# Four layer norms of a two-block network, computed half by half of the tokens, and a modulation sum moved to PSUM

## What is computed

```python
def second_block(x, c, ...):
    cond = jax.nn.silu(c)
    for l in range(2):
        mod = (cond @ ada_w[l] + ada_b[l])[:, None, :]
        sh_m, sc_m, g_m, sh_f, sc_f, g_f = jnp.split(mod, 6, axis=-1)
        h = x * (1.0 + sc_m) + sh_m
        y = even_mixer(h, ...) if l % 2 == 0 else odd_mixer(h, ...)
        x = layer_norm_2(DN_ALPHA * x + (1.0 + g_m) * y, ln_mix_g[l], ln_mix_b[l])
        h = x * (1.0 + sc_f) + sh_f
        y = conv_ffn(h, ffn_w_up[l], ffn_conv_w[l], ffn_w_down[l])
        x = layer_norm_2(DN_ALPHA * x + (1.0 + g_f) * y, ln_ffn_g[l], ln_ffn_b[l])
    return x

def layer_norm_2(x, g, b):
    mu = jnp.mean(x, axis=-1, keepdims=True)
    var = jnp.mean(jnp.square(x - mu), axis=-1, keepdims=True)
    return (x - mu) * lax.rsqrt(var + 1e-5) * g + b
```

## Time and profile before

| | us |
|---|---|
| median of 3 runs (2568.92 to 2570.44) | 2570.07 |
| the profiled execution's own time | 2565.9 |
| its span, first to last instruction | 2564.1 |
| PE busy in the span | 2471.4 (96%) |
| DVE, ACT, POOL busy | 1483.6, 1041.7, 1069.9 |

### The profile page before, as it was taken

The page is one execution under the profiler, slowest core; times in us unless marked ns, Lnnn a source line. Parts: engine busy times, 40 slices in busy tenths (PEclk is TensorE's granted clock), DMA queues, the critical chain, the costliest instruction groups (busy, mean ns, idle before and its releaser), DMA issues.

```text
span 2564.1 us, 30477 instructions
## 1 busy us (share of the span) xinstructions
PE 2471.4 (96%) x11318; PEld 1947.3 (76%) x11318; DVE 1483.6 (58%) x1904; ACT 1041.7 (41%) x1387; POOL 1069.9 (42%) x358
## 2 busy tenths in 40 slices
PE   7989999999999999999999998999998998999997
PEld 4658888887676788888876876888886756788886
DVE  6975756764455567477537775651654365652553
ACT  5564322235556642222434253532344343542333
POOL 5844444434343434444343423444435212444443
PEclk9999999999999999999999999999999999999999
DMA  5215545533222255465243312223323122224322
GB/s 147 67 58 164 186 148 183 181 91 114 83 58 75 61 178 181 145 192 169 86 129 99 99 50 74 83 78 111 98 75 98 58 70 66 72 78 121 94 78 67
DMA packets 397551, 273.37 MB, mean 107 GB/s; under 512 B 10067, under 2 KB 379731, under 8 KB 397436
## 3 DMA queue, kind: packets, MB, share of 16 engines
q1 hardware_dynamic: 383612, 221.52, 30.2%
q10 hardware_dynamic: 13824, 50.34, 5.3%
HBM read 269.70 MB, written 2.12 MB: 106 GB/s over the span
## 4 chain that ended last, share of the span: by engine, by line
PE 82%; ACT 5%; POOL 5%; DVE 4%; issue 3%; SPq 0%; DMA 0%; ACTq 0%; DVEq 0%; POOLq 0%
PE ps L688 25%; PE ps L690 25%; PE ps L689 25%; POOL act L2212 2%; POOL weight_lo L2175 2%; PE ps L1287 1%; ACT weight_hi L2310 1%; DVE act L1776 1%; PE ps L928 1%; PE ps L902 1%; PE ps L890 1%; PE ps L887 1%; ACT arena L2579 0%; DVE tmp L1604 0%; PE ps L1002 0%
## 5 line engine op out<-in xcount | busy, mean ns | idle before, releaser
L2175 POOL TENSOR_TENSOR weight_lo<-weight_raw,weight_hi 128x2048 fp32r<-128x2048 f32 (+2 forms) x223 | 917.4, 4114 | 1325.4 <-ACT weight_hi L2310 1323.5
L688 PE MATMUL ps<-u_hi,weight_hi 128*128 128x512 f32 x2312 | 915.9, 396 | 39.2 <-DVE u_lo L1395 29.2
L690 PE MATMUL ps<-u_hi,weight_lo 128*128 128x512 f32 x2328 | 910.5, 391 | 0.0
L689 PE MATMUL ps<-u_lo,weight_hi 128*128 128x512 f32 x2312 | 904.1, 391 | 0.0
L2310 ACT ACTIVATE weight_hi<-weight_raw 128x2048 fp32r<-128x2048 f32 (+2 forms) x223 | 381.3, 1710 | 543.2 <-PE ps L690 509.4
L688 PEld LDWEIGHTS ps<-u_hi,weight_hi 128*128 128x128 f32 x2312 | 436.9, 189 | 156.4 <-DVE u_lo L1395 35.1
L690 PEld LDWEIGHTS ps<-u_hi,weight_lo 128*128 128x128 f32 x2328 | 439.6, 189 | 92.9
L689 PEld LDWEIGHTS ps<-u_lo,weight_hi 128*128 128x128 f32 x2312 | 437.0, 189 | 92.7 <-issue 3.3
L688 PE MATMUL ps<-act_hi,weight_hi 128*128 128x512 f32 x704 | 274.3, 390 | 2.0 <-DVE act_lo L1361 2.0
L689 PE MATMUL ps<-act_lo,weight_hi 128*128 128x512 f32 x704 | 273.9, 389 | 0.0
L690 PE MATMUL ps<-act_hi,weight_lo 128*128 128x512 f32 x704 | 273.9, 389 | 0.0
(11 more groups left out here) (318 smaller groups left out, 2496.0 us busy)
## 6 DMA issues: line engine op xcount, KB each, us to landing
weight_raw<-in_ffn_w_up SPq DMA_DIRECT2D x132, 512.0 KB, 5.2
arena<-in_ada_w ACTq DMA_DIRECT2D x96, 512.0 KB, 5.8
weight_raw<-in_ffn_w_down SPq DMA_DIRECT2D x64, 704.0 KB, 4.7
weight_raw<-in_ffn_w_gate SPq DMA_DIRECT2D x44, 512.0 KB, 4.0
weight_raw<-in_ev_w_in SPq DMA_DIRECT2D x10, 1024.0 KB, 5.4
weight_raw<-in_conv_w_pw SPq DMA_DIRECT2D x16, 512.0 KB, 5.5
weight_raw<-in_ple_w_gate SPq DMA_DIRECT2D x16, 512.0 KB, 3.8
weight_raw<-in_attn_w_qkv SPq DMA_DIRECT2D x16, 512.0 KB, 5.2
```

The costliest lines, as they stand in the source:

```text
L688: pe.matmul(bank, w[0], x[0], start=start, stop=False)
L689: pe.matmul(bank, w[0], x[1], start=False, stop=False)
L690: return pe.matmul(bank, w[1], x[0], start=False, stop=stop)
L2175: pool.tensor_tensor(w_lo[r][:, 0:width], raw[r][:, 0:width], w_hi(k0 + j)[:, 0:width].bitcast(F32), ALU.subtract).then_inc(w_ready, 1)
```

## The change

1. **The last two tiles ahead of a seam** are computed by halves of 256 tokens (`token_halves`): tile 6 first half, tile 7 first half, tile 6 second half, tile 7 second half. The first half's statistics (`mean_stat`, `variance_stat`: three fp32 matmuls with ones on 256 tokens each) stand within tile 6's second half. The running sums end with chunk 5 instead of chunk 6.
2. **The layer norm** is done for the first 256 tokens and then for the others, on ACT, DVE and POOL, by instructions of half the width (`seam`). The second half's mean, root and table loads are put between the first half's operand chunks.
3. **The first two slots behind a seam** are computed half by half (`behind_seam`): for each half and each chunk, 12 matmuls on 256 tokens, for all four tiles. The second half's statistics stand behind chunks 0 and 1 of the first half. `fill` goes.
4. The high parts of these two slots get buffers of their own (`behind_hi`, in `arena`), so that they can be split before the seam; POOL makes both low parts ahead of centring. Slot 2 is split within the second half's operands.
5. ACT's `conv_taps` takes its first step out of the loop (`peel=1`); its tap copies then need no table load there.
6. At seam 3 the output leaves in 16 DMAs of 256 tokens instead of 8 of 512.
7. The modulation sum is kept in PSUM banks 6 and 7: two instructions of 512 for each of 1024, and two transposes for each.

```diff
-        ada_acc = arena[:, 0:D]
+        ada_acc = [ps[:, 6], ps[:, 7]]
...
+            def mean_stat(s, z):
+                cols = HALVES[z]
+                if z:
+                    pe.wait_ge(mean_neg, 2 * s + 1)
+                    pe.wait_ge(mean_free, s + 1)
+                pe.wait_ge(half_sums, s + 1)
+                pe.matmul(ps[:, 4, cols], ones, sum1[:, cols], start=True, stop=False)
+                for c in (DC - 2, DC - 1):
+                    if z == 0:
+                        pe.wait_ge(h_half, 2 * s + c - (DC - 3))
+                    else:
+                        pe.wait_ge(tile_used, BANKS + stages[SEAMS[s]][2] + c + 1)
+                    mm = pe.matmul(ps[:, 4, cols], ones, chunk(h, c)[:, cols], start=False, stop=c == DC - 1)
+                mm.then_inc(stat_half, 1)
...
+            def token_halves(s, w_of, x, kc):
...
+                def part(j, z, bank):
+                    cols = HALVES[z]
+                    for k in range(kc):
+                        hi, lo = x(k)
+                        mm = product(bank[:, cols], w_of(j, k), (hi[:, cols], lo[:, cols]), k == 0, k == kc - 1)
+                        if (j, z) == (0, 1):
+                            if k == 4:
+                                mean_stat(s, 0)
+                            if k == 6:
+                                variance_stat(s, 0)
+                    return mm
...
+            def behind_seam(name, behind=None):
...
+                order = [(j, k) for k in range(DC) for j in range(2)]
+                for z, cols in enumerate(HALVES):
+                    for at, (j, k) in enumerate(order):
+                        if j == 0:
+                            pe.wait_ge(x_half, 16 * s + 8 * z + k + 1)
...
+                        for i in range(2):
+                            mm = product(banks[j][i][:, cols], cols_of(w[j], i, k), (hi[:, cols], lo[:, cols]), k == 0, k == DC - 1)
+                            if z and k == DC - 1:
+                                mm.then_inc(tile_done, 1)
+                        if z == 0 and at == 1:
+                            mean_stat(s, 1)
+                        if z == 0 and at == 3:
+                            variance_stat(s, 1)
...
+                half_add(DC - 2, 0)
+                half_add(DC - 1, 0)
+                variance(0)
+                half_add(DC - 2, 1)
+                centre(0)
+                dve.wait_ge(root_half, 2 * s + 1)
+                scale(0, 0)
+                if mixer:
+                    first_low(0)
+                else:
+                    scale(1, 0)
+                half_add(DC - 1, 1)
+                for c in range(1 if mixer else 2, DC):
+                    scale(c, 0)
+                    if mixer and 2 <= c <= 4:
+                        low(c - 1, 0)
+                variance(1)
+                if mixer:
+                    for c in range(4, DC):
+                        low(c, 0)
+                centre(1)
+                dve.wait_ge(root_half, 2 * s + 2)
...
-                    if s == 0 and kk == 0:
-                        ada_link(dve.tensor_scalar(acc, ada_slot[kk], by, None, ALU.mult))
-                    else:
-                        ada_link(dve.scalar_tensor_tensor(acc, ada_slot[kk], by, acc, ALU.mult, ALU.add))
+                    for z, acc in enumerate(ada_acc):
+                        row = ada_slot[kk][:, z * S:(z + 1) * S]
+                        if s == 0 and kk == 0:
+                            ada_link(dve.tensor_scalar(acc, row, by, None, ALU.mult), 1 - z)
+                        else:
+                            ada_link(dve.scalar_tensor_tensor(acc, row, by, acc, ALU.mult, ALU.add), 1 - z)
...
+                for c in range(DC):
+                    operand(c, 0)
+                    if c == 0:
+                        square(DC - 1, 1)
+                    if c == 2:
+                        mean(1)
+                    if c == 3:
+                        ln_table_ahead()
+                    if c == 5:
+                        root(1)
+                for c in range(DC):
+                    operand(c, 1)
+                    if c == 3:
+                        split(next_slot + 2)
...
-                run_steps(sc, HC, body, 4, tail=2)
+                run_steps(sc, HC, body, 4, peel=1, tail=2)
```

More of the change, by code:

```diff
@@ L52 @@
 SLOT = 2048
+HALVES = (slice(0, S // 2), slice(S // 2, S))
+SEAMS = ("e_out", "down2b", "o_out", "down3b")
+BEHIND = {"up2a": 0, "o_in": 1, "up3a": 2}
 PARAM_WIDTHS = [
@@ L141, in plan_slots @@
     hi_free, last_use = [], [0] * HI_RING
+    apart = {stages["wo"][0] + 2} | {stages[name][0] + j for name in BEHIND for j in range(2)}
     for k in range(len(loads)):
-        third_wo = k == stages["wo"][0] + 2
-        hi_free.append(0 if third_wo else last_use[k % HI_RING])
-        if split_no[k] and not third_wo:
+        hi_free.append(0 if k in apart else last_use[k % HI_RING])
+        if split_no[k] and k not in apart:
             last_use[k % HI_RING] = tiles_after[k]
@@ L777, in stage_gemm @@
                 first = 2 if fill else 1
-                rest(name, body, (last if drain else last + 1) - first, first)
+                seam = SEAMS.index(name) if name in SEAMS else None
+                rest(name, body, (last if drain or seam is not None else last + 1) - first, first)
                 if drain:
                     drained()
+                if seam is not None:
+                    w = slot_of(name, Step(last))
+                    token_halves(seam, lambda i, k: cols(w, i, k), xu, DC)
             def rest(name, body, count, first=1):
@@ L808, in body @@
                     mm.then_inc(tile_done, 1)
-                run_steps(pe, DC, body, 4)
+                if seam is None:
+                    run_steps(pe, DC, body, 4)
+                    return
+                for j in range(DC - 2):
+                    body(Step(j))
+                w = [slot_of(name, Step(j)) for j in (DC - 2, DC - 1)]
+                token_halves(seam, lambda j, k: halves(w[j], lambda t: t[:, k * P:(k + 1) * P]),
+                             lambda k: (chunk(act_hi, k), chunk(act_lo, k)), HC)
             def rms_stat(adds=9):
@@ L1258, in _ @@
             stage_gemm("e_out", order=(4, 5, 6, 7, 0, 1, 2, 3))
[L1259 to L1263, removed]
+            behind_seam("up2a")
+            stage_down("down2a")
+            stage_gemm("up2b", wait=False)
+            stage_down("down2b")
             def lat_stats(chunks):
@@ L1320, in _ @@
             stage_gemm("o_out")
[L1321 to L1324, removed]
-            residual_stat("down3b")
-        operand_at = []
+            behind_seam("up3a")
+            stage_down("down3a")
+            stage_gemm("up3b", wait=False)
+            stage_down("down3b")
+            mean_stat(3, 1)
+            variance_stat(3, 1)
         @block.vector
```

381 lines of the change are left out of this document (256 added, 125 removed).

## The result

| | before | changed |
|---|---|---|
| median of the runs | 2569.49 (4 runs, 2564.89 to 2570.44) | 2603.29 (4 runs, 2598.08 to 2603.48) |
| profiled execution / span | 2565.9 / 2564.1 | 2598.1 / 2596.3 |
| PE, DVE, ACT, POOL busy | 2471.4, 1483.6, 1041.7, 1069.9 | 2492.2, 1493.8, 1065.7, 1068.8 |

A forecast was written before the change was run, and what follows sets the result against it. PE was taken as the bound, busy 2471.4 of 2564.1 us. Seams 0 and 2 (+1.5, +1.6), clock (+3.4), seam 1 (-2.0) and seam 3 (+0.9) gave +5.4 on 2570.07: 2575, with 8 in 10 from 2563 to 2584.

The forecast's parts named there:

- Nothing waits so far: Seam 0, tile 6's start to tile 7's second half ending at 14.1 us: PE meets no wait.
- Splits and DMAs of slots 0 and 1 are earlier and off the path: First two slots behind a seam: making them earlier costs nothing; only 0.48 us for `weight_lo` was waited there before.
- The third rival: More low clock and late slot 3, if DVE's multiplication slows beside POOL: 2583; chance 0.17, shared with small-operand cost.
- The half matmuls: PE at the seams: 0.120 us apart, 6.7 ns more per half; 1.9 us at seams 0 and 2, 2.2, 0.9.
- Statistics: PE at each seam: twelve fp32 matmuls on 256 columns make 5.2 us, against 3.4 for the four before.
- first operand's wait: Seams 0 and 2, after tile 7's second half: PE waits 1.8 us, 7.1 before; none at seam 1.
- new wait at slot 2: Seams 0 and 2: PE waits 3.3 us for the release of the bank of slot 0's first tile.
- the middle waits: Within the two slots behind a seam: PE's small waits for operand chunks, 3.4 us at seam 0, 3.3 at seam 1.
- The clock: Behind slot 2's wait at seams 0 and 2: 3.4 us at half clock, costing 1.7 us each.
- The 1.8 like the second: Seams 0 and 2: the 1.8 us idleness, like an earlier one of 1.7 us, is followed by no low clock.
- Seam 1: Interval to the end of slots 0 and 1: no first wait, 47.4 us plus some 0.8 against 50.3, -2.0 rounded.
- seam 3: From tile 6's start to the span's end: 33.0 us against 32.1, +0.9, through the first half's leftovers in ACT's queue.

The follow-up runs named there:

- e1: Changed kernel, but at seams 0 and 2 the gated product of a tile is written back into its own PSUM bank instead of SBUF: 2590.04 us, ratio 1.0076.
- e6: Changed kernel with a separate buffer for the last slot's high part (down2b, down3b); PE waits for slot 7 only at tile 7's first half: 2585.62 us, ratio 1.0067.
- e7: Changed kernel with the edits of e1 and e6 together: 2578.69 us, ratio 1.0027.
- e9: e7, and DVE does both shifted taps of a slot's first tile and frees its bank before turning to the second: 2573.6 us, ratio 1.0019.
- e11: e9 with DVE's second centring and chunk 0 scaling earlier, and ACT splitting slot 2 during its wait for the first variance: 2564.56 us, ratio 0.999.

## Why the prediction was wrong

- **"Nothing waits so far"** (seams 0 and 2) is the first step that failed. It took DVE's adds at their undisturbed 0.69 us and "Splits and DMAs of slots 0 and 1 are earlier and off the path" as free. The split is; POOL's two low parts that follow it, 9.6 us, aren't, since they hold DVE's add. Price: 3.04 us of wait and 1.7 us of low clock at each seam, of which e1 took back 54.0 - 49.2 = 4.8 at seam 0 and 54.1 - 49.5 = 4.6 at seam 2. The third rival had DVE slowed beside POOL, but for one multiplication near slot 3 only; the same wasn't asked of the adds that the change puts beside POOL.
- **Seams 1 and 3** failed, as the second step, by what wasn't asked: which weight the new order wants earlier. I followed the operands' chain and not the slots'. Price: 4.75 us each, with the low clock behind: 6.7 at seam 1 and 7.4 at seam 3 over the forecast, of which e6 gave back 6.5 and 7.3.
- **The half matmuls** were right: they follow each other by 0.12 us in the changed kernel too. An estimate by the rule of the Trainium skill that the prediction weighed (TensorE: Matmul & The Clock Gate, "Back-to-back issue gap") is 0.109; the measurement decides.
- **Statistics, first operand's wait** (1.81 and 1.75 for 1.8), **new wait at slot 2** (3.38 for 3.3) and **the middle waits** were right in place and nearly in size: 0.88 + 0.93 + 0.33 + 0.60 = 2.7 at seam 0, and 0.89 + 1.28 + 0.33 + 0.61 = 3.1 at seam 2, for 3.4. The waits of e1's two seams sum to 7.9 and 8.2 us for the 8.5 of the forecast, but each costs more than the idle time shown: 0.16 ahead of it, since a half matmul lasts 0.28 and the next one, which usually begins after 0.12, doesn't overlap it, and 0.1 behind it, since the matmul that waited is followed after 0.22. For a seam that is 1.5 us, for which the sum had no term; it makes up the 1.0 and 1.3 by which e1's seams exceed 48.2.
- **The clock**: behind slot 2's wait as forecast at seam 0, and for about twice as long at seam 2. "The 1.8 like the second", that is without effect, was too sharp. In e7 and e9 the 1.8 us at seam 0 were followed by 3.4 us at 0.50, in the changed kernel, e1 and e11 not.
- **Seam 1** would have been a gain of 1.8 us, as forecast (48.5 in e6 against 50.3), and **seam 3** a loss of 1.0 for 0.9 forecast.
- **The sum** of the parts that were priced is right to some 3 us (e7: 2578.7 for 2575); the rest, some 24 us, came from two causes at a price of nothing.

## What to carry to other kernels

When an edit asks for things in smaller or other pieces, list for each first use what is needed (operand, bank, both halves of the weight) and when it is made: the halved tile wants its neighbour's weight after 4.0 us instead of 7.5. When it moves work of one engine, look what runs on the others at the new place; a row whose maximum or mean lies far over its minimum in the old profile hints at an instruction that an engine's neighbour can hold up. A wait that covers two things should stand where the second is first used.

## What the runs showed of the hardware

- A DVE instruction with both inputs in SBUF, begun beside one of POOL's `low_halves`, ends 0.3 (256 columns) to 0.55 us (512) after it: 5.03 us for 0.69, 2.62 for 0.42. With one input in PSUM it isn't held (0.69 beside POOL, e1; 0.757 at most in 168 instructions of the modulation sum).
- Idleness of 1.8 us ahead of the first operand on PE is followed by the lower clock in some executions and not in others; 3.0 us and more were followed by it at every seam of every kernel here. One such stretch is 3.4 us and costs 1.7; behind slot 2's wait at seam 2 it was about twice that, and the stretch between seams 2 and 3 grew by 2.8.
- Taking 3.4 us of wait down to 1.65 (e9) was worth more than the wait, since the low clock behind it went with it: 2.0 us in seam 0's interval and 0.6 in the stretch behind it, for 1.7 of wait.
